# Slots unrolled one by one with small background pieces between them, diagonals on ScalarE, gathers with constant waits

## The reference, cut to what matters

```python
sc, pos = lax.top_k(cand, PEER_TOPK)
eidx = jnp.take_along_axis(cidx, pos, axis=-1)
g = jax.nn.softmax(sc, axis=-1)
u = jnp.take(expert_u, eidx, axis=0)
a = jnp.einsum('thkd,td->thk', u, hc).astype(jnp.float32)
act = (jax.nn.gelu(a, approximate=False) * g).astype(hc.dtype)
vv = jnp.take(expert_v, eidx, axis=0)
return jnp.einsum('thk,thkd->td', act, vv)
```

## Time and profile before

| | us |
|---|---|
| three executions: median | 2008.4 |
| the profiled execution: span | 2007.8 |
| attention of block 1, up to the first gather | 316 |
| phase 0, to 703 | 387 |
| phase 1, to 1190 | 487 |
| phase 2, to 1656 | 466 |
| phase 3, to 1998 | 342 |
| last norm and output | 10 |

### The profile page before, as it was taken

How to read it: one execution, slowest core, us unless ns; L and a number is a source line. 1 busy time by engine, 2 the same in 40 slices (tenths; PEclk the granted TensorE clock), 3 DMA queues, 4 the chain that set the end, 5 groups by cost and what they waited for, 6 DMA issues and landing times.

```text
span 2007.8 us, 20033 instructions
## 1 busy us (share of the span) xinstructions
PE 1483.5 (74%) x5550; PEld 885.4 (44%) x5550; DVE 1334.4 (66%) x2996; ACT 431.5 (21%) x978; POOL 1076.6 (54%) x1574
## 2 busy tenths in 40 slices
PE   8979997775565667698777867788877765665665
PEld 7968775552222245344434524545444432222222
DVE  5652226889898736443775676576776588778675
ACT  2247421112111121421122122222211211121111
POOL 5520005556666736254644654555465567776994
PEclk9989999987777898799887978899878888877888
DMA  6612238998999988778769987988878999999997
GB/s 254 246 63 68 102 126 322 370 368 344 372 368 359 375 353 354 318 283 344 305 248 368 391 355 295 402 330 349 323 286 320 385 354 399 371 377 367 413 422 291
DMA packets 89125, 639.55 MB, mean 319 GB/s; under 512 B 10033, under 2 KB 10562, under 8 KB 11986
## 3 DMA queue, kind: packets, MB, share of 16 engines
q0 software_dynamic: 73728, 536.90, 67.4%
q1 hardware_dynamic: 13248, 94.38, 12.0%
q10 hardware_dynamic: 2066, 7.24, 1.1%
HBM read 637.43 MB, written 1.05 MB: 318 GB/s over the span
## 4 chain that ended last, share of the span: by engine, by line
PE 43%; DVE 26%; POOL 11%; DMA 9%; issue 7%; ACT 4%; POOLq 0%; DVEq 0%; ACTq 0%
PE acc L933 15%; PE bank L465 10%; DVE ring L1773 10%; DMA ring<-in_experts,slot_idx 8%; POOL ring L976 6%; POOL slot_idx L972 4%; PE bank L477 4%; PE bank L519 3%; DVE diag L1761 2%; DVE X L1767 2%; PE bank L451 1%; PE bank L551 1%; DVE pick_tmp L1525 1%; DVE pick_tmp L1535 1%; DVE pick_tmp L1523 1%
## 5 line engine op out<-in xcount | busy, mean ns | idle before, releaser
L933 PE MATMUL acc<-ring,diag 128*128 128x512 f32 x1536 | 804.0, 681 | 434.8 <-DVE diag L1761 434.7
L933 PEld LDWEIGHTS acc<-ring,diag 128*128 128x128 f32 x1536 | 324.1, 218 | 893.0 <-DVE diag L1761 548.2
L1773 DVE CUSTOM_DVE_ANT_0 ring<-ring,hn 128x1024 f32<-128x1024 f32 x512 | 621.6, 1221 | 124.6 <-DMA ring<-in_experts,slot_idx 118.3
L976 POOL DMA_INDIRECT ring<-in_experts,slot_idx x512 | 611.7, 1195 | 80.3 <-issue 8.4
L972 POOL COPY slot_idx<-eidx 128x1 uint32 (+1 forms) x512 | 232.4, 454 | 741.0 <-PE acc L933 534.0
L1339 ACT ACTIVATE act_dot<-dot 128x1 f32<-128x1 f32 x512 | 101.5, 202 | 920.8 <-DVE dot L1773 920.7
L1761 DVE TENSOR_SCALAR diag<-const,act_dot,gates 128x128 f32<-128x128 f32 x384 | 131.5, 343 | 141.2 <-ACT act_dot L1339 141.2
L465 PE MATMUL bank<-wring,hT 128*128 128x256 f32 (+1 forms) x896 | 214.8, 400 | 2.5 <-ACT hT L1082 1.4
L465 PEld LDWEIGHTS bank<-wring,hT 128*128 128x128 f32 (+1 forms) x896 | 172.1, 195 | 40.3 <-issue 6.0
L975 POOL TENSOR_TENSOR fence<-fence 128x1 f32<-128x1 f32 x512 | 166.3, 325 | 41.3
L1767 DVE SCALAR_TENSOR_TENSOR X<-ring,weight,X 128x1024 f32<-128x1024 f32 x128 | 165.4, 1292 | 4.6
(11 more groups left out here) (222 smaller groups left out, 1232.2 us busy)
## 6 DMA issues: line engine op xcount, KB each, us to landing
wring<-in_weights SPq DMA_DIRECT2D x88, 1024.0 KB, 9.3
ring<-in_experts,slot_idx POOLq DMA_INDIRECT x512, 9.9
ring<-in_na_bias ACTq DMA_DIRECT2D x1, 1536.0 KB, 7.4
gain<-in_gain ACTq DMA_DIRECT2D x3, 512.0 KB, 5.3
const<-in_const ACTq DMA_DIRECT2D x1, 1472.0 KB, 6.8
X<-in_x SPq DMA_DIRECT2D x2, 512.0 KB, 4.3
out<-hn SPq DMA_DIRECT2D x2, 512.0 KB, 5.4
ring<-in_dil_mask ACTq DMA_DIRECT2D x1, 768.0 KB, 4.2
```

The source lines that it names most:

```text
L933: ins = nc.tensor.matmul(acc[:, half, :], diag[:, s, :], ring[:, s, D + half * 512:D + (half + 1) * 512], start=False, stop=False)
L976: nc.gpsimd.indirect_dma_start(out=ring[:, s, :], out_offset=None, in_=table, in_offset=bass.IndirectOffsetOnAxis(ap=slot_idx[:, s:s + 1], ...
L1773: nc.vector.tensor_tensor_reduce(out=u, in0=u, in1=hn[:, t, :], scale=1.0, scalar=0.0, op0=ALU.mult, op1=ALU.add, accum_out=dot[:, s:s + 1 ...
```

## The change

- The loops are gone: every engine's stream has each of the 512 slots written out, with constants in its waits. The background of every engine is cut into pieces (a `yield` in its step ends one; 196 on TensorE, 130 on ScalarE, 335 on VectorE), and a digit of `TURNS` says how many of the next pieces stand ahead of a slot (`h` is 17, `f` 15, `d` 13). The order of the pieces is that of before, but for the step `close`.
- A slot on ScalarE is now gelu, then the weight, then the diagonal, each waiting for the one before. VectorE makes no diagonals and no weights.
- In phases 0 and 3 all slots go to TensorE. In phases 1 and 2 slots with n % 4 == 1 go to VectorE, which adds them two slots later.
- GpSimd issues the gather straight from `eidx`, with one wait per ring place (`slot_free0` to `slot_free7`), without copy and fence.
- `acc` is opened and closed by the first and last slot's matmul instead of by matmuls with zeros. Adding it to `X` is a background piece `close` of the next phase: before slot 1 of phase 1; before slot 0 of phases 2 and 3, behind the picks that stand there.
- By the digits, VectorE has before slot 63 of phase 0 three pieces of one pick, a key pick, and five pieces of the next pick. Before slot 0 of phase 2 it has `pick_keys` and `pick` of phase 2 group 0, `close` and the norm `ple1`. Before slot 0 of phase 3 it has `pick` of phase 3 group 0, `close` and four fifths of a key pick. Its half of the last residual add of phase 1 stands before slot 125, that of phase 2 before slot 117.

```diff
-ITERS = SLOTS // RING
-DVE_SLOTS = (3, 7)
-PE_SLOTS = tuple(s for s in range(RING) if s not in DVE_SLOTS)
+DVE_EVERY = (0, 4, 4, 0)
...
+DVE_LAG = 2
...
+TURNS = {
...
+    "dve": (
+        "011031122111100021111111311010003111112101111100020111111112101d",
+        "1110111111111112011102101111112101111000000000000000000000000000",
+        "0100010101000000000102011200000000000300010100000130000000000000",
+        "0000000003100001001102110200000101010211021101100200000001000120",
+        "h020011102000011111221200302000011200511011102010220040000010412",
+        "0111041102110021013000000111021102030102000000000100012000000311",
+        "f102111111011111111111201110210111111210111101000000000000000000",
+        "0000000000000000000000000000000000000000000000000000000000000000",
+    ),
+}
...
+        PLAN = [[step for g in range(1, PICKS) for step in (("query1", g), ("pick_keys", 0, g), ("pick", 0, g))]
+                + [("norm_rows", "meta"), ("norm_cols", "meta")] + pick_steps(1, 0),
+                [("close", 0)] + block2_steps(0),
+                [("close", 1)] + block2_steps(1),
+                [("close", 2)] + pick_steps(3, 1) + [("final", 0)]]
+        def on_dve(phase, n):
+
+            return DVE_EVERY[phase] and n % DVE_EVERY[phase] == 1
...
+        class Background:
...
+            def turn(self, phase, n):
+
+                for _ in range(int(self.turns[phase * SLOTS + n], 36)):
+                    next(self.todo)
...
@@ TensorE
-                for half in range(2):
-                    nc.tensor.matmul(acc[:, half, :], zeros, decay[:, 0:512], start=True, stop=False)
...
+                for n in range(SLOTS):
+                    background.turn(phase, n)
+                    if on_dve(phase, n):
+                        continue
...
+                    s = n % RING
+                    pe.wait_ge(sem("diag_ready"), pe_before[phase] + pe_slots[phase].index(n) + 1)
+                    for half in range(2):
+                        ins = nc.tensor.matmul(acc[:, half, :], diag[:, s, :], ring[:, s, D + half * 512:D + (half + 1) * 512],
+                                               start=(n == 0), stop=(n == SLOTS - 1))
+                    ins.then_inc(sem(free_after(phase, n)[0]), 1)
@@ GpSimd
-                nc.gpsimd.tensor_copy(slot_idx[:, s:s + 1], eidx[:, tile, bass.ds(i * RING + s, 1)]).then_inc(sem("idx_copied"), 1)
-                pool.wait_ge(sem("idx_copied"), it * RING + s + 1)
-
-                nc.gpsimd.tensor_tensor(fence[:, :], fence[:, :], fence[:, :], ALU.add)
...
+                for n in range(SLOTS):
+                    if n % PICK_SLOTS == 0:
+                        pool.wait_ge(sem("experts_picked"), phase * PICKS + n // PICK_SLOTS + 1)
+                    k = phase * SLOTS + n
+                    s = k % RING
+                    if k >= RING:
+                        pool.wait_ge(sem(f"slot_free{s}"), k // RING)
+                    nc.gpsimd.indirect_dma_start(
+                        out=ring[:, s, :], out_offset=None, in_=table,
+                        in_offset=bass.IndirectOffsetOnAxis(ap=eidx[:, tile, n:n + 1], axis=0)).then_inc(sem(f"row_in{s}"), 16)
@@ ScalarE
+                for n in range(SLOTS):
+                    background.turn(phase, n)
+                    k, s = phase * SLOTS + n, n % RING
+                    act.wait_ge(sem("dots"), k + 1)
+                    nc.scalar.activation(act_dot[:, s:s + 1], dot[:, s:s + 1], ACT.Gelu).then_inc(sem("gelu"), 1)
+                    act.wait_ge(sem("gelu"), k + 1)
+                    nc.scalar.activation(weight[:, s:s + 1], act_dot[:, s:s + 1], ACT.Copy, scale=gates[:, t, n:n + 1]).then_inc(sem("weighted"), 1)
+                    if not on_dve(phase, n):
+                        act.wait_ge(sem("weighted"), k + 1)
+                        nc.scalar.activation(diag[:, s, :], ident, ACT.Copy, scale=weight[:, s:s + 1]).then_inc(sem("diag_ready"), 1)
@@ VectorE
+                for n in range(SLOTS):
+                    background.turn(phase, n)
+                    s = n % RING
+                    dve.wait_ge(sem(f"row_in{s}"), ((phase * SLOTS + n) // RING + 1) * 16)
+                    u = ring[:, s, 0:D]
+                    nc.vector.tensor_tensor_reduce(out=u, in0=u, in1=hn[:, t, :], scale=1.0, scalar=0.0, op0=ALU.mult, op1=ALU.add,
+                                                   accum_out=dot[:, s:s + 1]).then_inc(sem("dots"), 1)
+                    if n >= DVE_LAG and on_dve(phase, n - DVE_LAG):
+                        accumulate(phase, n - DVE_LAG)
```

More of the change, by code:

```diff
@@ new lines, in pick_steps @@
+        def pick_steps(phase, first):
+            return [step for g in range(first, PICKS) for step in (("pick_keys", phase, g), ("pick", phase, g))]
+        PLAN = [[step for g in range(1, PICKS) for step in (("query1", g), ("pick_keys", 0, g), ("pick", 0, g))]
[3 more added lines that the diff above has]
+                [("close", 2)] + pick_steps(3, 1) + [("final", 0)]]
@@ new lines, in on_dve, with free_after, __init__, parts @@
+        def on_dve(phase, n):
+            return DVE_EVERY[phase] and n % DVE_EVERY[phase] == 1
+        pe_slots = [[n for n in range(SLOTS) if not on_dve(phase, n)] for phase in range(PHASES)]
+        pe_before = [sum(len(s) for s in pe_slots[:phase]) for phase in range(PHASES)]
+        def free_after(phase, n):
+            k = phase * SLOTS + n
+            return f"slot_free{k % RING}", k // RING + 1
+        class Background:
+            def __init__(self, engine, steps):
+                self.engine = engine
+                self.turns = "".join(TURNS[engine])
+                self.steps = steps
+                self.todo = self.parts()
+            def parts(self):
+                for phase in range(PHASES):
+                    for name, *where in PLAN[phase]:
+                        if name in self.steps:
+                            made = self.steps[name](*where)
+                            if made is not None:
+                                yield from made
+                            yield
+            def turn(self, phase, n):
+                for _ in range(int(self.turns[phase * SLOTS + n], 36)):
+                    next(self.todo)
+            def rest(self):
+                for _ in self.todo:
+                    pass
@@ L416, in build, with whole @@
+        def whole(step):
+            for _ in step:
+                pass
         block = ctx.enter_context(nc.Block())
@@ L634, in query1 @@
             def query1(g):
-                w = [unit() for _ in range(PAIR_HEADS)]
+                w = []
                 for t in range(TILES):
                     if g == 0:
-                        norm(f"ffn{t}")
+                        whole(norm(f"ffn{t}"))
                         drained(pe, (f"ffn{t}", 1))
@@ L1738, in final, with close @@
                 norm(f"f{t}")
+            def close(phase):
+                t = PHASE_TILE[phase]
+                name, n = free_after(phase, SLOTS - 1)
+                dve.wait_ge(sem(name), n)
+                added = [k for k in range(SLOTS) if on_dve(phase, k)]
+                if added:
+                    name, n = free_after(phase, added[-1])
+                    dve.wait_ge(sem(name), n)
+                rows = X[:, t, :].rearrange("p (h d) -> p h d", h=2)
+                nc.vector.tensor_tensor(rows, rows, acc[:, :, :], ALU.add).then_inc(sem("x_ready"), 1)
             STEPS = {"pick_keys": pick_keys, "pick": pick, "norm_rows": norm, "norm_cols": norm_cols, "ple_up": ple_up,
@@ L1742, in _, with accumulate @@
                      "gla_start": gla_start, "gla_qk": gla_qk, "gla_heads": gla_heads, "gla_end": gla_end,
-                     "mixed_rows": mixed_rows, "out2": out2, "final": final}
-            def background(steps):
-                for name, *where in steps:
-                    if name in STEPS:
-                        STEPS[name](*where)
+                     "mixed_rows": mixed_rows, "out2": out2, "final": final, "close": close}
+            background = Background("dve", STEPS)
+            def accumulate(phase, n):
+                t, s = PHASE_TILE[phase], n % RING
+                dve.wait_ge(sem("weighted"), phase * SLOTS + n + 1)
+                nc.vector.scalar_tensor_tensor(out=X[:, t, :], in0=ring[:, s, D:], scalar=weight[:, s:s + 1], in1=X[:, t, :],
+                                               op0=ALU.mult, op1=ALU.add).then_inc(sem(free_after(phase, n)[0]), 1)
@@ L1783, in _ @@
+                for n in range(SLOTS - DVE_LAG, SLOTS):
+                    if on_dve(phase, n):
+                        accumulate(phase, n)
+            background.rest()
+            close(PHASES - 1)
             norm("f1")
```

318 lines of the change are left out of this document (153 added, 165 removed).

## The result

The changed kernel takes 1833.41 us (median of four, 1827.22 to 1836.40) against 2008.40 before: a ratio of 0.9126, 95% interval 0.9107 to 0.9146. The forecast was 1848, a gain of 160 us where 175 were measured.

What follows compares the result with a forecast made beforehand. Bound: gathered bytes at 416 GB/s (1425 of 1682 us) plus idle DMA while the ring starves for free slots. Stage savings of 32, 59, 60 and 9 us sum to 160: span 2007.8 to 1847.8, forecast 1848, range 1795 to 1955.

Steps and rivals of the forecast that it cites:

- the loop stretch: Stretch of the old kernel where only the slot loop runs: DMA share 1.01, 416 GB/s, 2.52 us a slot.
- Stage 0: First of four passes over 128 gathered expert slots: 341 + 7 + 7 = 355 us forecast, 32 less than before.
- The 13 pieces: VectorE's background before slot 63 of the first pass: about 12.6 us, costing some 7 with 5 us of slack.
- Stage 1: Second pass over 128 slots: 395 us for slots plus 33 at its end, 428 forecast, 59 less.
- The jostle: Loss where TensorE's work and DMA transfers run side by side: 9 us in the second pass, 8 in the third.
- The stage's end: Chain with nothing beside it, from last residual add to next pass's first index: 33 us, bounds 20 and 45.
- Stage 2: Third pass: 381 us transfers, 7 first landing, 10 last pick, 8 for engines in each other's way: 406, minus 60.
- Stage 3: Fourth pass: 317 us transfers, 7 for an empty ring, 9 for tail and extra pieces: 333, minus 9.
- Slack: Ring turn falls from 18 to 15.3 of 20 us covered; unseen stalls grow from some 2 to some 5 us.
- TensorE's clock: Rival: low clock in first and last passes, 3.6 us a slot, 507 and 466 us there, 2133 in all; chance 0.05.
- a bound chain: Rival: background chain stays the bound in the two middle passes, 472 and 451 us, 1937 in all; chance 0.19.
- All hidden: Rival: second pass's end costs its lower bound, nothing jostles, block before slot 63 covered: 1794 us; chance 0.13.

Runs made afterwards that it cites:

- the spread pieces: Changed kernel with key scores of two picks moved to slots 66 and 80, and VectorE's 13 pieces spread one to a slot over slots 63 to 110: 1813.54 us.

## Why the prediction was right, point by point

**The bound.** Right. Bytes at the rate of the loop stretch plus idle DMA gave the frame, and with the spread pieces stage 0 runs at share 1.01 from 330 us to its end. The four stages now move 142, 158, 158 and 135 MB, 593 in all, as forecast, and the time in which the DMA engines are busy is as forecast too. The best stretches run at 422 GB/s, but over all busy time the rate is 417, next to the 416 of the earlier trace rows. Nearly the whole miss is in the idle time (us; idle in windows of 2 us as above, transfers the rest of the stage):

| | transfers, forecast | found | idle DMA, forecast | found |
|---|---|---|---|---|
| stage 0 | 341 | 340 | 14 | 20 |
| stage 1 | 386 | 382 | 42 | 28 |
| stage 2 | 381 | 378 | 25 | 20 |
| stage 3 | 317 | 323 | 16 | 10 |
| sum | 1425 | 1422 | 97 | 78 |

**Stage 0**, 355 forecast, 359.5 measured: two errors that partly cancel, which is luck. The first landing costs 2 us instead of 7, and the hole around slot 63 costs 18 instead of 7. The 13 pieces do last 12.1 us (12.6 forecast), but the step "With 5 us of slack it costs some 7 us" failed. It costed the 13 pieces and did not ask why they stand there. They must: TensorE's key scores before slot 55 take a PSUM bank that VectorE gives back in exactly these pieces, slot 55 stands behind them, and row 63 can only come when slot 55 has gone. Moving two digits gave 12.6 us in that stage. This wait is in no row of the trace of before; it follows from counting bank turns over the pieces.

**Stage 1**, 428 and 409.7. The jostle, guessed at 9 us, is 6.5: so much DMA is idle in the stage ahead of its end. TensorE's work took 348.8 us instead of 369.7 as its granted clock rose from 0.86 to 0.93. The stage's end was put at 33 us, and this term is the largest miss. The gap in the gathers is about that long, but the DMA share in it is 0.59 and 0.60 for 20 us: weights for the next steps use it, which the forecast named and did not subtract. Idle DMA is 23.6 us, of which 22 fall into this stage.

**Stage 2**, 406 and 397.9. The jostle (8 us) is not there: between the holes at its two ends 0.7 us of DMA is idle. Its end, 10 us in the sum and 10 to 20 among the signs, has 19.2. **Stage 3**, 333 and 332.5: it moves 135 MB instead of 132, which takes 6 us more, and has 6 us less of idle DMA; that these cancel is luck. In sum +4.5, -18.3, -8.1 and -0.5 make -22.4: 1847.8 to 1825.4 us.

**Slack.** The mechanism is supported, and its number was low. That the diagonal's move is worth more than that of copy and fence (31 against 5 us, the 5 within the uncertainty) fits what the turn round the ring says, 1.8 us against 0.8. The block of 12.1 us on VectorE alone left 4.9 us of DMA idle, so about 7 us passed unseen where the forecast had "some 5 us".

**ScalarE.** The bounds for a diagonal (266 to 343 ns) and a weight (202 ns) missed: 401 and 295 ns. The nearest rows had a copy without a factor per partition. The count was off too: 448 diagonals move there, not 416 (128 + 96 + 96 + 128). Diagonals and weights take 331 us where the forecast had 230. The Trainium skill (ScalarE: Activation LUTs, What ACT_TABLE_LOAD costs) has a formula for it: 186 ns plus 0.833 ns for each column, and some 93 ns for each pointer operand, that is an estimate of 386 and 280 ns, near both. 134 table loads lie behind 316 us, 132 were counted ahead. That this was hidden fits ScalarE's 44% of the span.

**TensorE's clock**, the rival on the slower side, stayed away. Four matmul records of a slot now take 1.98 us with a gap of half a microsecond before each slot, and the granted clock of stage 3 is 0.98, that is 2.4 GHz almost throughout. The trace of the changed kernel, and below it that of the kernel before in the same kind of stretch:

```profile
1755.50 1.98 PE L1018 MATMUL acc<-ring,diag 128*128 128x512 f32 x4 [0.50 <-ACT diag L1406]
1757.99 1.98 PE L1018 MATMUL acc<-ring,diag 128*128 128x512 f32 x4 [0.51 <-ACT diag L1406]
```

```profile
1869.74 7.11 PE L933 MATMUL acc<-ring,diag 128*128 128x512 f32 x12 [3.37 <-DVE diag L1761]
```

Before, a gap of 3.37 us (a slot of VectorE among those of TensorE) preceded 12 records in 7.11 us instead of 5.42. Not every such gap did: of the 13 gaps of 2.6 to 3.5 us between 1857 and 1990 us, nine were followed by records at a lower rate and four (3.52, 2.60, 3.02 and 2.98 us) were not. All slots on TensorE made it faster, the opposite of the rival: TensorE's work in stages 0 and 3 was forecast at 318 and 285 us and took 289.5 and 256.5. The run with a quarter of the slots back on VectorE shows the same from the other side (clock 0.87, 572 ns a record).

**The other rivals.** With a bound chain, stages 1 and 2 were to take 472 and 451 us; they took 409.7 and 397.9, and few short holes are left in them. All hidden (1794) wanted the end of stage 1 at 20 us (22 found), no jostle (6.5 found in stage 1) and the block before slot 63 covered, where the 18 us of the bank wait stood.

**Signs to look for.** Stage 3's share and pitch, both holes at the stage ends and the table loads came as said. Three did not. Stage 0 has share 0.96 and 396 GB/s, not above 0.97 and near 410: that is the bank wait. TensorE's idle time for diagonals in stages 1 and 2 was to be gone and is 65.6 us, 181.2 before. And GpSimd's wait for slots there was to fall below 200 us. It is 241.8 + 143.8 = 386 us, about as long as before. An engine that issues for a full ring waits for slots when the DMA engines are the bound as well. VectorE's wait for rows (31.5 to 161.0) and the DMA share are the ones that tell.

## What to carry to other kernels

When a ring of transfers starves, measure the share of the DMA engines by stage and spread the other work over single slots before speeding up a slot: that was worth two to three times as much here. For each piece moved in an in-order stream, count also the buffer turns it takes, and ask why an odd clump stands where it does; here the wait behind the clump showed in no row until the new kernel ran. A wait of the issuing engine is no proof of starvation, and a full DMA share is no proof of the full rate.

## What the runs showed of the hardware

TensorE kept 2.4 GHz almost throughout stage 3 (granted 0.98) with regular gaps of 0.5 us in 2.5, while nine of 13 gaps of 2.6 to 3.5 us in the kernel before were followed by records at a lower rate. With gaps of some 3 us in every 10, in the run with a quarter of the slots on VectorE, the stage has 0.87. One core's DMA engines moved 8 KB rows gathered by index at 421 GB/s over the last 331 us of stage 0, in the run with the spread pieces. And no gain of streams written out in full shows: the kernel with all but the unrolling taken back has 17158 instructions where the looped one has 20033, and takes 24 us longer, for reasons that stayed open.
